# A decoder layer on one core: the head loop turned by two projection tiles, and key rotation put ahead of the selection rounds

## What is computed

```python
q, k, v, ga, qi, ki, wi, u, gb = _project(x, pos, w_in)     # one projection, w_in is 2048 x 7248
# indexer: scores of every key for every query, top 128 (prompt) or 256 (samples) kept
scores = einsum('bths,bth->bts', relu(qi . ki), wi) * scale
_, idx = lax.top_k(scores, topk)
# attention of 8 heads x 128 over the kept keys only; q and k rotated in the first 32 dims
s = einsum('bthd,btkhd->bthk', q, k_sel) * (HEAD_DIM ** -0.5)
o = einsum('bthk,btkhd->bthd', softmax(s), v_sel)
# beside it a pooling mixer over u; both are gated by silu, then
h = DEEPNORM_ALPHA * x + mixed @ w_out
y = layer_norm(h)
```

## Time and profile before

| | |
|---|---|
| median of 3 runs | 1297.9 us |
| lowest and highest | 1293.49, 1302.2 us |
| the profiled execution | 1295.51 us, its span 1293.7 us |
| mean granted TensorE clock | 0.969 of full speed |
| TensorE, matmuls busy | 1203.6 us (93% of the span), 10300 instructions |
| VectorE busy | 589.1 us (46%) |
| ScalarE busy | 358.1 us (28%) |
| GpSimd busy | 348.5 us (27%) |

### The profile page before, as it was taken

The page is one execution under the profiler, slowest core; times in us unless marked ns, Lnnn a source line. Parts: engine busy times, 40 slices in busy tenths (PEclk is TensorE's granted clock), DMA queues, the critical chain, the costliest instruction groups (busy, mean ns, idle before and its releaser), DMA issues.

```text
span 1293.7 us, 27396 instructions
## 1 busy us (share of the span) xinstructions
PE 1203.6 (93%) x10300; PEld 1104.7 (85%) x10300; DVE 589.1 (46%) x1079; ACT 358.1 (28%) x663; POOL 348.5 (27%) x150
## 2 busy tenths in 40 slices
PE   7899976989899999989998999999999989999995
PEld 6788755989899999989997888887988869999992
DVE  3455569986128405730862432432522624232326
ACT  4232331213223312332232323222232323212110
POOL 2322210323243324223431212112221213333320
PEclk9899978989999999999999999999999989999996
DMA  8522230323133223313326677677667765222203
GB/s 247 141 67 72 58 88 1 99 74 91 51 99 91 74 75 99 91 51 99 91 74 215 225 238 240 234 242 245 233 234 238 235 200 198 82 81 82 80 0 138
DMA packets 197976, 170.56 MB, mean 132 GB/s; under 512 B 19890, under 2 KB 178538, under 8 KB 196658
## 3 DMA queue, kind: packets, MB, share of 16 engines
q1 hardware_dynamic: 184458, 160.48, 40.2%
q10 hardware_dynamic: 13424, 8.67, 2.3%
HBM read 159.47 MB, written 9.74 MB: 131 GB/s over the span
## 4 chain that ended last, share of the span: by engine, by line
PE 75%; DVE 12%; issue 8%; ACT 2%; DMA 2%; DVEq 0%; ACTq 0%; SPq 0%
PE acc L1003 55%; PE bank L1217 5%; PE bank L1234 3%; PE acc L1285 2%; PE bank L1060 2%; DVE scoreP L1534 2%; DVE top L1530 2%; PE bank L1163 2%; PE bank L1144 1%; PE acc L1339 1%; DVE rot L1461 1%; DVE top L1569 1%; DVE scoreS L1572 1%; DVE y L1872 1%; DMA xnat<-in_x_prompt 1%
## 5 line engine op out<-in xcount | busy, mean ns | idle before, releaser
L596 POOL TENSOR_TENSOR wL<-rawW,wH 128x1024 fp32r<-128x1024 f32 (+1 forms) x146 | 348.3, 2387 | 896.8 <-ACT wH L618 896.8
L1003 PE MATMUL acc<-actH,wH 128*128 128x272 f32 (+1 forms) x2336 | 503.4, 297 | 11.7 <-issue 8.7
L1003 PE MATMUL acc<-actH,wL 128*128 128x272 f32 (+1 forms) x2336 | 487.8, 291 | 0.8 <-issue 0.8
L1003 PE MATMUL acc<-actL,wH 128*128 128x272 f32 (+1 forms) x2336 | 486.8, 290 | 0.0
L1003 PEld LDWEIGHTS acc<-actH,wH 128*128 128x128 f32 (+1 forms) x2336 | 371.0, 191 | 33.1 <-issue 30.9
L1003 PEld LDWEIGHTS acc<-actL,wH 128*128 128x128 f32 (+1 forms) x2336 | 371.7, 191 | 0.0
L1003 PEld LDWEIGHTS acc<-actH,wL 128*128 128x128 f32 (+1 forms) x2336 | 369.1, 191 | 0.9 <-issue 0.9
L618 ACT ACTIVATE wH<-rawW 128x1024 fp32r<-128x1024 f32 (+1 forms) x146 | 153.9, 1055 | 270.9 <-PE acc L1003 260.7
L1217 PE MATMUL bank<-sq,kPage 128*128 128x128 f32 x512 | 69.9, 280 | 9.5 <-issue 5.4
L1217 PEld LDWEIGHTS bank<-sq,kPage 128*128 128x128 f32 x512 | 56.0, 142 | 21.9 <-issue 16.8
L1828 DVE SCALAR_TENSOR_TENSOR y<-y,bank 128x512 f32 x16 | 11.0, 688 | 133.8 <-PE bank L1398 133.8
(11 more groups left out here) (198 smaller groups left out, 992.7 us busy)
## 6 DMA issues: line engine op xcount, KB each, us to landing
rawW<-in_w_in SPq DMA_DIRECT2D x112, 512.0 KB, 3.8
kPage<-in_cache_k SPq DMA_DIRECT2D x64, 512.0 KB, 4.6
vPage<-in_cache_v SPq DMA_DIRECT2D x64, 512.0 KB, 4.8
rawW<-in_w_out SPq DMA_DIRECT2D x32, 512.0 KB, 3.9
y<-in_x_prompt SPq DMA_DIRECT2D x4, 1024.0 KB, 8.6
out_y_prompt<-y SPq DMA_DIRECT2D x8, 512.0 KB, 2.8
xnat<-in_x_prompt SPq DMA_DIRECT2D x2, 1024.0 KB, 7.6
xnat<-in_x_prompt ACTq DMA_DIRECT2D x2, 1024.0 KB, 11.4
```

Of the source, the lines that this page charges most:

```text
L596: pool.tensor_tensor(wL[:, slot, :, 0:width], rawW[:, slot, :, 0:width], wH[:, slot, :, 0:width].bitcast(F32), ALU.subtract).then_inc(stag ...
L1003: last = pe.matmul(acc[t.slot][0:width, e, 0:HT], w[:, u.slot, k, 0:width], a[:, kk, e * HT:(e + 1) * HT], start=(kk == 0 and w is wH and ...
```

## The change

TensorE, ScalarE and the bank table: the head loop is turned by two tiles. The two value tiles of the first pair and the transposes of v0 stand ahead of the loop; a pass now runs over the tiles `TILE_C + 2` to `TILE_C + 9`, so the last two are the value tiles of the next pair, and the second head's `turned` and `values_of` stand between their halves. The loop makes three passes; the last pass is written out behind it, and has two quarters of tile B (`TILE_B`, half 0) in the places of the missing value tiles. These two quarters are taken out of the page phase. The wait for the copied values moves from `values_of` to `scores`. SyncE's loads keep their order.

VectorE: in each pass the three rounds ahead of `rotated(3, kT, 0)` go; four rounds instead of three stand ahead of `rotated(4, qT, 0)`; the softmax of the first head comes behind the next two as before, and two more rounds stand between it and `rotated(5, kT, 1)`. Its loop keeps its four passes.

In `group`, the transposes of the second output, `output_turned("b")`, come ahead of the last quarter instead of behind it.

```diff
@@ values of the next pair use the last two places of the bank table
+        cp = banks.stage(["v0", "vs0"], (6, 7))
+        cl = banks.stage(["v1", "vs1", "k0", "ks0", "S00", "S10", "S20", "S30", "k1", "ks1", *c_uses(0),
+                          "S01", "S11", "S21", "S31", *c_uses(1), "v0", "vs0"], four, 4)
...
@@ ScalarE
+                    if j == 8:
+                        probs_turned(1, (0, 1))
+                    if j == 9:
+                        values(0, cl("v0", i), cl("vs0", i), i + 1)
...
-                    if j == 7:
-                        probs_turned(1, (0, 1))
+                    if j == 8:
+                        probs_turned(1, (2, 3))
...
@@ TensorE
+            unit(TILE_C, 0)
+            unit(TILE_C, 1)
+            unit(TILE_C + 1, 0)
+            copied(TILE_C)
+            by_token(cb("v0"), cb("vs0"), raw[:, 0])
+            unit(TILE_C + 1, 1)
...
+                unit(TILE_C + 7, 1, i, 8)
+                if last:
+                    unit(TILE_B, 0, quarters=(0,))
+                else:
+                    unit(TILE_C + 8, 0, i, 8)
                 turned(1, 0)
                 turned(1, 1)
+                if last:
+                    unit(TILE_B, 0, quarters=(1,))
+                else:
+                    unit(TILE_C + 8, 1, i, 8)
                 values_of(1, 0)
                 turned(1, 2)
                 values_of(1, 1)
                 turned(1, 3)
+                if not last:
+                    unit(TILE_C + 9, 0, i, 8)
                 values_of(1, 2)
                 values_of(1, 3)
+                if not last:
+                    copied(TILE_C + 8, i, 8)
+                    by_token(cl("v0", i), cl("vs0", i), raw[:, 0])
+                    unit(TILE_C + 9, 1, i, 8)
+
+            with pe.Fori(0, 3) as i:
+                heads(i, False)
+            heads(3, True)
...
@@ the page phase
-                if m in (0, 2, 4, 5):
-                    quarter((0, 0, 1, 1, 2, 3)[m])
+                if m in (2, 5):
+                    quarter(2 + m // 5)
...
@@ group
+                output_turned("b")
+                if not last:
                     quarter(20, g)
-                output_turned("b")
...
@@ VectorE
                 make_gate(0)
-                pick_keys(3)
                 rotated(3, kT, 0)
-                pick_keys(3)
+                pick_keys(4)
                 rotated(4, qT, 0)
+                pick_keys(2)
+                softmax(0)
                 pick_keys(rounds - 6)
-                softmax(0)
                 rotated(5, kT, 1)
```

More of the change, by code:

```diff
@@ L351, in c_uses, with cb @@
             return [f"{u}{X}" for u in ("P0", "P1", "O0", "P2", "O1", "P3", "O2", "O3")]
-        cb = banks.stage(["v0", "vs0", "v1", "vs1", "k0", "ks0", "S00", "S10", "S20", "S30", "k1", "ks1",
-                          *c_uses(0), "S01", "S11", "S21", "S31", *c_uses(1)], four, 4)
+        cp = banks.stage(["v0", "vs0"], (6, 7))
+        cl = banks.stage(["v1", "vs1", "k0", "ks0", "S00", "S10", "S20", "S30", "k1", "ks1", *c_uses(0),
+                          "S01", "S11", "S21", "S31", *c_uses(1), "v0", "vs0"], four, 4)
+        for b in (6, 7):
+            banks.used[b] -= 1
+        def cb(name, i=None):
+            if name in ("v0", "vs0"):
+                return cp(name) if i is None else cl(name, i, ago=1)
+            return cl(name, i)
         def key_uses(X, lo=0, hi=16):
@@ L778, in probs_turned @@
                         out_of(b, probT[:, t % 2, 0:t + 1, :].rearrange("p s t -> p (s t)"), src[:, 0:(t + 1) * P])
-                for j in range(8):
+                for j in range(2, 8 if last else 10):
                     high(TILE_C + j + 2, 0, i, 8)
-                    if j in (1, 2):
-                        values(j - 1)
+                    if j == 2:
+                        values(1, cb("v1", i), cb("vs1", i), i)
                     if j == 3:
@@ L1127, in _, with by_token, heads @@
             full(b, pe.transpose(take(b)[0:NS, 0:NS], scoreSTn[:], ident[0:NS, 0:NS]))
-            with pe.Fori(0, 4) as i:
-                def by_token(name, X, src):
-                    b = cb(f"{name}{X}", i)
-                    dst = take(b)
-                    for t in range(TT):
-                        last = pe.transpose(dst[:, t * P:(t + 1) * P], src[:, t * P:(t + 1) * P], ident)
-                    full(b, last)
-                    b = cb(f"{name}s{X}", i)
-                    full(b, pe.transpose(take(b)[0:NS, 0:P], src[:, NP_:T], ident))
+            def by_token(b, b2, src):
+                dst = take(b)
+                for t in range(TT):
+                    last = pe.transpose(dst[:, t * P:(t + 1) * P], src[:, t * P:(t + 1) * P], ident)
+                full(b, last)
+                full(b2, pe.transpose(take(b2)[0:NS, 0:P], src[:, NP_:T], ident))
+            unit(TILE_C, 0)
[4 more added lines that the diff above has]
+            unit(TILE_C + 1, 1)
+            def heads(i, last):
                 def scores(X):
+                    bv = cb(f"v{X}", i)
+                    pe.wait_ge(bank_free[bv.slot], bv.read)
                     for t in range(TT):
@@ L1156, in values_of @@
                 def values_of(X, t):
-                    bv, bp, b = cb(f"v{X}", i), cb(f"P{t}{X}", i), cb(f"O{t}{X}", i)
+                    bp, b = cb(f"P{t}{X}", i), cb(f"O{t}{X}", i)
                     dst = take(b)
-                    pe.wait_ge(bank_free[bv.slot], bv.read)
                     pe.wait_ge(bank_free[bp.slot], bp.read)
@@ new lines, in heads @@
+                unit(TILE_C + 4, 1, i, 8)
+                unit(TILE_C + 5, 0, i, 8)
+                pe.wait_ge(head_ready, 4 * i + 3)
+                scores(0)
+                unit(TILE_C + 5, 1, i, 8)
+                unit(TILE_C + 6, 0, i, 8)
+                keys_by_token(1)
+                turned(0, 0)
+                turned(0, 1)
+                unit(TILE_C + 6, 1, i, 8)
+                values_of(0, 0)
+                turned(0, 2)
+                values_of(0, 1)
+                turned(0, 3)
```

92 lines of the change are left out of this document (46 added, 46 removed).

## The result

| | kernel before | changed kernel |
|---|---|---|
| median (lowest to highest) | 1297.07 us (1293.49 to 1302.2), 4 runs | 1320.32 us (1316.17 to 1323.26), 4 runs |
| ratio | | 1.0162, 95% interval 1.0133 to 1.0191 |
| profiled execution, its span | 1295.51, 1293.7 us | 1316.17, 1314.4 us |
| mean granted TensorE clock | 0.969 | 0.961 |
| TensorE, matmuls busy | 1203.6 us | 1209.4 us |

The change makes the kernel 1.6% slower by the recorded ratio. The medians lie 23.2 us apart, which is 1.8%; the recorded ratios are not the quotients of the medians and differ from them by up to 0.2 points. The two profiles lie 20.7 us apart. The forecast was 1309, range 1299 to 1318. The direction and most steps hold; the time lies above the range.

The account below looks back on a forecast made before the run. TensorE, busy nearly throughout, was taken as the bound, with VectorE in step and without slack between kT and second kT. The terms sum to +11.7 us: 1307.2 profiled, 1309.6 as median; stated 1309, range 1299 to 1318.

Parts of the forecast that it names:

- The rounds: Head loop: VectorE's moved selection rounds delay TensorE 6.2 us a pass, at scores and second keys; four passes, +24.8 us.
- The clock: Head loop: TensorE's granted clock falls after each new stop at the second keys, 1.8 us each; four, +7.2 us.
- The first rotation: First head-loop pass: TensorE's wait for kT goes, gaining 5.5 us and 2.2 for the clock; -7.7 us.
- The loop turned: waits of 1.1 us: Head loop: the four waits for the second head's copied probabilities get half a tile as cover; -4.3 us.
- The loop turned: returns: Head loop: two returns at 1.8 us, without a clock fall, replace three costing about 13.4 us together; -9.8 us.
- Tail and page phase: Two quarters of tile B move from page phase to last tail, which lengthens; page phase loses cover; together +0.5 us.
- Output transposes, group returns: Group loop: reordered output transposes wait for a copy, about +0.3 us in three groups; returns unchanged; +1.0 us.
- B: Last rotation slips past GpSimd's subtraction, or the clock does not fall after the new stops; 1300 to 1302 us, chance 0.12.
- E: Added rounds find room on VectorE between scores and second keys and cost nothing; 1278 us, 1.5% faster, chance 0.08.
- Rival C: Head-loop returns are not covered and cost as before, with more clock and page-phase loss; 1316 to 1319 us, chance 0.18.
- Rival D: TensorE's queue of 64 instructions covers the whole branch, 4.0 us, so the head-loop returns vanish; 1306 us, chance 0.05.

Follow-up runs that it names:

- quarters back: Changed kernel with the two quarters of tile B moved from the last pass's tail back between the key pages; 1319.2 us, ratio 1.0173.
- the kernel of five things with the loop kept: Changed kernel with three rounds behind second kT rotation, output transposes back, last key pages loaded earlier, 25 TensorE increments at two places; 1280.5 us, ratio 0.9875.
- written out, all together: Changed kernel, head loop written out, three rounds behind second kT rotation, output transposes back, key pages earlier, 30 increments at three places; 1277.3 us, ratio 0.9831.

## Why the prediction was right or wrong

By its own steps, profile to profile:

| step | forecast | measured |
|---|---|---|
| The rounds | +24.8 | +25.0 (20.3 + 5.1 less the 0.4 of the old waits) |
| The clock | +7.2 | +7.3 |
| The first rotation | -7.7 | -7.9 |
| The loop turned: waits of 1.1 us | -4.3 | -4.3 |
| The loop turned: returns | -9.8 | -3.7 |
| Tail and page phase | +0.5 | +0.6 (quarters back) |
| Output transposes, group returns | +1.0 | +2.2 (1.7 and 5.9 for 5.4) |
| sum | +11.7 | +19.2 |

The profiles differ by 20.7, so 1.5 are left over. By stages, the last transposes ahead of the head loop start 1.4 us later and the output projection takes 0.8 us longer (230.2 for 229.4), both in parts that the change doesn't touch; against that the steps of the table add up to 0.9 us more than the head loop and its tail took (20.1 for 19.2), and to 0.2 us less than the page phase and the groups (-0.9 for -0.7). The profiled execution of the changed kernel is the fastest of its four, 4.1 us under their median, where the forecast had added 2.4. So 1309.6 + 7.5 + 1.5 + 1.7 = 1320.3.

**The rounds, the clock, the first rotation** were right, in size and in mechanism, and the runs that take them apart confirm them. Only the credit for the first rotation is shared: with the old order of rounds the turned loop alone has a first stop of 1.1 us for 5.7, so most of that gain needs either change and not both. Rivals B and E fall: the rotation did meet GpSimd's subtraction, the clock did fall, and VectorE had no room in that stretch.

**The step that failed is "The loop turned"**, its term for the returns. "I take 1.8 without a fall of the clock: 2 x 1.8 = 3.6" was measured at 9.7. How far the branch runs ahead was right (2.3 us). Its duration was not. I took 3.6 us from the old loop, with one packet at the branch, though I had written down a branch of 5.0 in the group loop and made it only a bound. The signs that I had named, a branch of 3.5 to 5 us and 1.5 to 3 us idle, were just missed at the first return (5.3 and 3.3 us). The term's upper bound, 3.0 us and 1.7 of clock for each, gives -4.0, and -3.7 was measured. With the code moved by 100 places, and in the kernel of five things with the loop kept, the stops were 1.56 to 1.69 us without a fall of the clock. So the step failed by something that neither the edit nor the order of instructions shows: where in its 16 KB blocks the loop's end had come to lie. Rival C came closest with 1316 to 1319 (its terms add up to 1315 to 1319), and it was right that each return would cost about as much as before (4.8 us; it had said 4.5). But its reason, returns that are not covered, did not hold, since 2.3 us of work did cover each branch; and its upper end took in 1.6 us of clock and 2.5 us in the page phase that were not there. So it came close in part by luck.

**Tail and page phase** was right as a sum and wrong in both parts: I forecast 6.0 us more in the tail and 5.5 less in the page phase, and got 3.7 and 3.1 (by the run with the quarters back). The quarters cover a wait of 2.1 us in the tail, and the page phase can't shrink by all that is taken out of it, since the last key pages land when they land. Its check, "shorter by about 5.5 us", failed for that reason: from the second transposes to the fifth quarter it took 25.8 us before and 23.4 after.

**The queue.** Rival D, the Trainium skill's queue of 64 instructions, stays without support: in the head loop the branch was issued 2.2 to 2.3 us ahead of the last matmul's end at every return of the turned loop, in all profiles, never 4.

**The range** ended just under rival C's upper end. With the measured steps the prediction's own sum is 1317.1. What took the median past 1318 are the 1.5 us left over and the distance from profile to median, 1.7 us more than before, for neither of which the range held anything.

## What to carry over

Look where the engine that others wait for is in step with them, and put its free work elsewhere: three of eight rounds cost 30 us or nothing by their place alone. Moving code can cost even where it moves no work, because a loop's branch may come to lie on the fetch of the next block; so compare the branches of all loops after any edit, of loops that you haven't touched too, and shift the code by some tens of instructions in a place where the engine waits. Work taken out of a phase that loads bound comes back in part as a wait.

## What the runs showed of the hardware

- A branch back over several blocks of code takes 3.3 to 3.9 us in one loop and 3.8 to 5.5 in another with one instruction packet, and 4.6 to 6.6 with two that start close together. At the head loop's returns a packet alone takes 1.0 to 1.4 us; the second of two close together takes 1.5 to 2.4 in either loop.
- A taken branch can cost twice: 1.7 us of work after a return TensorE stood still for another 3.40 us, at a place in the code that moved with the shift and is taken for the end of the target's block.
- In the head loop the granted clock fell behind stops of 2.5 to 3.4 us at the returns in most cases (not behind one of 2.52 and one of 2.94), and not behind those of 1.56 to 1.69 us (four of four). There a shorter stop saves more than its length: 3.3 us became 1.6, and 1.8 of clock went too. In the group loop the length of the stop does not decide it: the clock stayed at 1.00 behind stops of 3.15 us (changed kernel) and 3.30 us (quarters back), and was 0.83 over the 10 us behind one of 2.09 us (written out, all together).
- A semaphore increment on TensorE takes about 0.1 us of its time where nothing covers it: 12.8 us for 100 at the program's start (0.13 each), and stops of 3.0, 2.7 and 1.9 us for 32, 30 and 25 behind a wait (0.08 to 0.09 each).
- The loop saved no fetches: 9 packets of 16 KB start between two returns of the head loop, and the whole program has 71 packets for 76 once that loop is written out.
- A product of 32 x 544 on VectorE took 2.85 us beside GpSimd's subtraction and 0.71 alone, in the changed kernel as before.
